# Expert loop: the spreading of finished rows moved ahead of the second block's gate/up products

## What is computed

```python
def expert_block(args):
    xe, e = args
    return (jax.nn.silu(xe @ w1[e]) * (xe @ w3[e])) @ w2[e]

yb = lax.map(expert_block, (xb, block_e)).reshape(P, D)
y = jnp.zeros((T, D), jnp.float32).at[buf_tok].add(yb.astype(jnp.float32) * buf_w[:, None])
```

## Time and profile before

| | us |
|---|---|
| median of 3 runs | 1916.44 |
| lowest, highest | 1915.33, 1916.66 |
| profiled execution | 1916.96 |
| its span in the profile | 1915.2 |
| TensorE busy | 1868.0 (98%) |
| VectorE busy | 573.8 (30%) |
| ScalarE busy | 465.9 (24%) |

### The profile page before, as it was taken

The page is one execution under the profiler, slowest core; times in us unless marked ns, Lnnn a source line. Parts: engine busy times, 40 slices in busy tenths (PEclk is TensorE's granted clock), DMA queues, the critical chain, the costliest instruction groups (busy, mean ns, idle before and its releaser), DMA issues.

```text
span 1915.2 us, 21829 instructions
## 1 busy us (share of the span) xinstructions
PE 1868.0 (98%) x8178; PEld 933.1 (49%) x8178; DVE 573.8 (30%) x1045; ACT 465.9 (24%) x813; POOL 177.2 (9%) x216
## 2 busy tenths in 40 slices
PE   8999999999999999999999999999999999999997
PEld 4555888646463333333334443686453333333333
DVE  2254556332141322313223103312241322313223
ACT  4254333242331111111113014323331111111112
POOL 2000333030100000000001000121100000000001
PEclk9999999999999999999999999999999999999998
DMA  6210100035089999999995113104089999999992
GB/s 188 88 45 6 40 1 1 23 117 193 0 314 423 423 425 423 422 423 423 424 423 212 46 44 109 67 1 179 0 321 422 424 424 422 423 423 424 423 424 117
DMA packets 88415, 465.77 MB, mean 243 GB/s; under 512 B 22304, under 2 KB 24464, under 8 KB 47403
## 3 DMA queue, kind: packets, MB, share of 16 engines
q1 hardware_dynamic: 77600, 450.98, 58.1%
q0 software_dynamic: 4608, 7.92, 1.1%
q10 hardware_dynamic: 6154, 6.15, 1.0%
HBM read 467.59 MB, written 6.29 MB: 247 GB/s over the span
## 4 chain that ended last, share of the span: by engine, by line
PE 81%; DMA 11%; DVE 4%; ACT 1%; POOL 1%; issue 1%; SPq 0%; DVEq 0%; ACTq 0%; POOLq 0%
PE ps L1040 74%; DMA W<-in_moe_w 11%; PE ps L1248 2%; PE ps L1711 1%; PE ps L1682 1%; DVE memN L1835 0%; DVE XI L2023 0%; PE ps L1185 0%; PE ps L1472 0%; DVE XJ L1964 0%; PE ps L1053 0%; DVE gcs L2132 0%; DVE KKt L1997 0%; DVE XT L2304 0%; DVE gsn L2163 0%
## 5 line engine op out<-in xcount | busy, mean ns | idle before, releaser
L1040 PE MATMUL ps<-W,xgT 128*64 128x512 f32 x2048 | 453.9, 595 | 6.3 <-DMA W<-in_moe_w 5.0
L1040 PE MATMUL ps<-HT,W 128*128 128x512 f32 (+2 forms) x896 | 337.7, 534 | 5.1 <-DVE XT L1842 1.7
L1040 PEld LDWEIGHTS ps<-W,xgT 128*64 128x64 f32 x2048 | 143.7, 137 | 287.1 <-issue 272.0
L1040 PEld LDWEIGHTS ps<-HT,W 128*128 128x128 f32 (+1 forms) x896 | 166.5, 189 | 164.4 <-issue 148.5
L2291 DVE TENSOR_TENSOR XT<-ps,XT 128x512 f32<-128x512 f32 x240 | 166.0, 692 | 239.6 <-PE ps L1040 239.6
L1040 PE MATMUL ps<-W,act 128*64 128x512 f32 x1024 | 231.9, 596 | 0.0
L1040 PE MATMUL ps<-spread,ysb 128*128 128x512 f32 x512 | 228.3, 599 | 2.2 <-issue 2.2
L1040 PEld LDWEIGHTS ps<-spread,ysb 128*128 128x128 f32 x512 | 94.8, 190 | 135.2 <-issue 134.8
L2283 DVE TENSOR_TENSOR act<-ps,sl 128x256 f32<-128x256 f32 x64 | 26.9, 420 | 446.0 <-ACT sl L991 446.0
L1040 PEld LDWEIGHTS ps<-W,act 128*64 128x64 f32 x1024 | 70.6, 137 | 133.4 <-issue 133.4
L987 ACT ACTIVATE hs<-ps 128x512 f32<-128x512 f32 x64 | 38.2, 597 | 387.2 <-PE ps L1040 387.2
(11 more groups left out here) (412 smaller groups left out, 1727.4 us busy)
## 6 DMA issues: line engine op xcount, KB each, us to landing
W<-in_moe_w SPq DMA_DIRECT2D x256, 1024.0 KB, 18.1
W<-in_moe_w SPq DMA_DIRECT2D x64, 2048.0 KB, 19.2
W<-in_od_w_in SPq DMA_DIRECT2D x6, 2048.0 KB, 8.7
W<-in_ev_w_in SPq DMA_DIRECT2D x3, 2048.0 KB, 8.0
W<-in_xa_wq SPq DMA_DIRECT2D x2, 2048.0 KB, 8.9
W<-in_xa_wo SPq DMA_DIRECT2D x2, 2048.0 KB, 12.0
hrows<-hk ACTq DMA_DIRECT2D x8, 512.0 KB, 11.8
W<-in_od_w_out SPq DMA_DIRECT2D x2, 2048.0 KB, 10.3
```

The costliest lines, as they stand in the source:

```text
L1040: return te.matmul(o, l, r, start=first, stop=last)
```

## The change

`add_pair` with its waits for `y_in` and `spread_in` moves from behind `up(1, i)` to ahead of it. The last wait of the group, for `add_in` (that banks 0 and 1 have been added), stays ahead of `turn_rows`.

```diff
                     turn_hidden(0, i)
-                    up(1, i)
                     if not first:
 
                         pe.wait_ge(s["y_in"], i * 2 + (pairs * 2 + 1))
                         pe.wait_ge(s["spread_in"], i + pairs)
                         add_pair(lambda k: pe.wait_ge(s["add_in"], i * 8 + (pairs * 8 + (k - 1))))
+                    up(1, i)
+                    if not first:
                         pe.wait_ge(s["add_in"], i * 8 + (pairs * 8 + 8))
                     turn_rows(i * 16 + (pairs * 16 + 16))
```

## The result

The changed kernel takes 1947.24 us (median of 4 runs, 1941.86 to 1953.14) against 1916.55 for the kernel before (4 runs, 1915.33 to 1926.64): a ratio of 1.0156, with an interval from 1.0133 to 1.018. It is slower by some 30 us, as forecast. The profiled execution of the changed kernel took 1953.14 us, with a span of 1951.3.

A forecast was written before the change was run, and what follows sets the result against it. TensorE was taken to bound the kernel, with the weight stream close behind. Thirty trips growing 1.21 us each, less 6.8 us of weight waits, gave +29.5 us on 1916.96: 1946.5 us, range 1935 to 1954.

The forecast's parts named there:

- What bounds the kernel: Expert loop: TensorE sets trips of 29.86 us; the weight stream's pace, 30.64 us, makes it wait late in a layer.
- The wait that comes out: Ahead of the moved spreading: TensorE stands still 0.80 us a trip until ScalarE's copy into ysb ends.
- The register steps: From the end of ScalarE's copy to the first spread product: register instructions behind the wait, taken as 0.35 us a trip.
- my two ends: Bounds for copy's end to first product: 0.04 us (total +20.2 us) and 0.45 us (total +32.5 us).
- The tile change: Turning of gathered rows now stands behind narrow products: 1.46 us to the down products instead of 1.40, 0.06 a trip.
- The cover of the hidden rows: Second block's hidden-row copy (0.60 us), now covered by eight transposes alone: costed at nothing, 0.2 us to spare.
- the dearer rival: Cover of the hidden rows fails, or register instructions between spread products are exposed: 0.3 us a trip, 1955.5 us; 8 in 100.
- The transfers: Second block's gate/up weights released 8.1 us later; landings some 8 us shorter after request, nothing lost, share slightly under 1.
- The 6.8 us: TensorE's waits for weights, 4.9 us in the first layer and 1.9 in the second, given back by trips of 31.07 us.
- The faster rival: ysb ready in time, exposed wait under 0.17 us a trip, down weights next to be late: -3.5 us, 1913.5; 4 in 100.
- No difference: Exposed wait of 0.1 to 0.36 us a trip cancels the waits for weights, within 3.8 us; 5 in 100.
- The sum: 30 trips times 1.21 us, 36.3, less 6.8 us of weight waits: +29.5 us, 1946.5 us.

The follow-up runs named there:

- pad_before: Kernel before, with the eight transposes of the gathered rows done twice in each trip and no step moved: 1939.59 us, ratio 1.0124.
- fewer_changes: Kernel before, with the transposes of the first block's hidden rows moved behind the second block's gate/up products, ahead of the spreading: 1918.48 us, ratio 0.9994.
- copy_twice_before: Kernel before, with ScalarE's two copies of the second block's finished rows made twice in each trip: 1917.62 us, ratio 1.0008.
- copy_twice_after: Changed kernel, with ScalarE's two copies of the second block's finished rows made twice in each trip: 2022.25 us, ratio 1.0541.
- copy_three_after: Changed kernel, with one more 0.59 us piece of ScalarE's copy ahead of the report of the finished rows: 1963.03 us, ratio 1.0225.
- first_half: Changed kernel, with the first four spread products waiting only for the first of ScalarE's two copies, the last four for the second: 1923.71 us, ratio 1.0037.
- wait_last: Changed kernel, with the wait for ysb placed behind the other waits, last ahead of the first spread product: 1940.79 us, ratio 1.0118.
- split: Kernel with transposes of the first block's hidden rows and spreading between the two halves of the second block's gate/up products: 1915.69 us, ratio 0.9998 to before.
- small_first: Changed kernel, with ScalarE's copy in pieces of 128, 384 and 512 features, each spread product waiting only for its piece: 1917.17 us, ratio 0.9986.

## Why the prediction was right

**What bounds the kernel** held: TensorE, with the stream close behind. pad_before and fewer_changes show both sides of it, a longer trip without waits and a shorter one that gives all back to them.

**The wait that comes out** held to 0.01 us. The transposes start at 1528.61 and need 0.50 by the prediction, the copy ends at 1529.92: 0.81, where the sum has 0.80. copy_twice_before, copy_twice_after, copy_three_after and first_half show the cause.

**The register steps** were the term that was mis-sized: 0.35 taken, 0.27 measured in the second layer and 0.12 in the first (30 x 0.35 = 10.5 against 15 x 0.39 = 5.9 us). They lay between my two ends. I took the value near the place behind the loops, because there too the wait stands on a register instruction. What I did not count is how many instructions stand from the released one up to the load: three behind the loops, but two in the second layer's loop and one in the first's, as the traces of the changed kernel and of wait_last show.

**The tile change** (0.06) came out as a number: 1.46 us from 1544.27 to 1545.73. Its reason did not. The changed order has as many tile changes as the one before, and split, with the same 1.46 and no idle, has trips of 29.82 us. The prediction took over 6.97 us for the spreading from its old place behind narrow products; in its new place behind wide transposes it would have taken 6.96 with the step back to narrow tiles included, instead of 7.05. The slower start behind the idle, about 0.1 us, made up for it, by luck. **The cover of the hidden rows** (nothing) held. With the measured steps a trip grows by 0.80 + 0.12 + 0.06 = 0.98 and 0.80 + 0.27 + 0.06 = 1.13; the marks give 1.00 and 1.14. No gap stands ahead of the second block's hidden rows (1544.27 to 1545.20, 0.93 us as in the earlier trace rows), so the dearer rival falls.

**The transfers.** The landings did get shorter. The requests for the second halves of the second block's gate/up weights in this trip (issued at 1544.5 and 1544.9):

```profile
DMA to landing us min/median/max: 7.5/8.8/10.2
```

The earlier trace rows has 17.7 to 20.5 for these, so they came down by some 10, where about 8 was forecast. The stream had that in hand: no wait for weights is left. Windows from the first mark of the first loop to its last, before and after, have the share fall a little under 1, as forecast:

```profile
569.12:1022.05 452.93, 449.32 (x1923) 171.51 (x1921) 117.08 (x178) 65.46 (x121) 18.04 (x30) 1.00 1.00 416
...
578.68:1041.59 462.91, 451.16 (x1923) 170.78 (x1921) 119.51 (x180) 64.89 (x120) 17.96 (x30) 1.00 0.98 407
```

The 6.8 us were given back, as pad_before shows for trip length alone.

**The faster rival** put two statements on record. That the down weights of the second block are next, small_first bears out: its trips in the first layer lose 1.8 us to them, where 1.5 was said, and those in the second layer none. In split, which releases only the second halves later, the first halves are next instead. That there is little to be had, both bear out: 4.2 us in the loops of small_first and 2.4 in those of split, where 3.5 was said. Its condition, an exposed wait under 0.17 us, is not met by the changed kernel. **No difference** was put at up to 0.36 us of exposed wait. That is (6.8 + 3.8) / 30 = 0.35 for the whole growth of a trip, with the 0.06 of the sum left out; and its lower end, 0.1, lies under the 0.17 up to which the faster rival was to hold. first_half tries the place: its trips are 0.47 us longer than 29.86 (the list of waits shows 0.25 a trip, because the ends of the products ahead are modelled), and its ratio of 1.0037 (1.0021 to 1.0052) stands for some 7 us, over that edge.

**The sum.** The forecast was 30 x 1.21 - 6.8 = +29.5. The loops give 15 x 1.00 + 15 x 1.14 - 6.8 = +25.3, measured +25.1. The medians say +29.9 to +30.7. So 1946.5 stands close to 1947.24 partly by luck: the register steps were 4.6 us too dear in it, and 4.8 to 5.6 us lie outside the loops, where nothing was forecast. Of these the traces show only that two of the three profiles of the changed kernel have some 413 us between the loops, at a lower granted clock, where the two of before have 408.2 and 409.5. pad_before has 412.1 there, 0.9 of it a doubled turning; its ratio stands for 23.8 us, where its loops and the two turnings outside them give 19.4 + 1.7 = 21.1, inside its interval of 20.3 to 27.4. wait_last (408.5) and first_half (407.6), with the changed order, have nothing of the kind. Whether the pace of the loop has a part in the clock of what follows, or this is scatter, stays open.

## What to carry to other kernels

Ahead of moving a step that reads another engine's result, subtract: the end of that result less the end of what now stands between, plus the steps between the released wait and the load (here 0.04 us with the wait on the load itself, 0.12, 0.27 and some 0.44 with one, two and three instructions) and some 0.1 for the start behind an idle, and multiply by the trips. Count those steps in the trace of the very place, not in the program text; if what is waited for comes in pieces, wait for the first piece alone (first_half got back 23 of 31 us, small_first all). Where two bounds are 1 to 3% apart, as TensorE and the stream are here, a gain on one is lost to the other (fewer_changes), and a loss is softened by it (pad_before). Compare loops between marks in the trace as well as medians: here the marks repeat to 0.2 us, while executions of one kernel differ by 10 and more.

## What was not expected of the hardware

- Idles of 2.01 and 2.15 us in each trip of a loop that is otherwise full cost 1.69 us more through the granted clock (0.60 in the 2.2 us behind the idle, 0.73 in the next 3) in 24 of 30 trips. Idles of 0.78 to 1.55 us brought no loss of clock.
- From the end of ScalarE's copy to the weight load it took 0.12 us with one TensorE instruction between (first loop), 0.27 with two (second loop, the same text), 0.43 to 0.46 with three (behind the loops), and 0.04 with the wait on the load itself (wait_last, second loop).
- The first product behind an idle was recorded with 0.69 us, behind work of the same tile width (split) with 0.60, and the trip was longer by as much.
- The granted clock in one stretch of the same instructions (180 to 300 us) was 0.91 in some executions and 0.99 in others, of either kernel, worth some 9 us.
- Two changes between full and narrow tiles fewer in a trip went with 0.34 us less (29.86 against 29.52, fewer_changes).
